# Two denominator groups a job, one ones product per norm in the FFN stages, and conv modulation weights outside the weight ring

## The reference

```python
for i in range(2):
    mod = silu(c) @ mod_w[i] + mod_b[i]              # six parts: shift, scale, gate, twice
    u = rms_norm(h, g) * (1 + scale) + shift
    y = conv_mixer(u) if i == 0 else attention(u)    # i==0: (b * conv3(c * x)) @ w_out
    h = h + gate * rms_norm(y, g)
    u = rms_norm(h, g) * (1 + scale2) + shift2
    f = (silu(conv3(u @ w_up)[g]) * conv3(u @ w_up)[up]) @ w_down
    h = h + gate2 * rms_norm(f, g)
```

## Time and profile before

| | |
|---|---|
| median of 3 runs | 2504.2 us (2503.1 to 2543.51) |
| the profiled execution | 2507.53 us; its slowest core, core 6, spans 2506.5 us |
| spans of the cores | 2487.3 to 2506.5 us |
| PE busy | 2361.9 us, 94% of the span |
| DVE, ACT, POOL busy | 1573.4, 1348.9 and 1193.9 us |
| DMA moved | 231.93 MB written, mean 93 GB/s |
| mean granted clock of the PE | 0.988 to 0.995 by core |

### The profile page before, as it was taken

One profiled execution on the slowest core, in us unless ns is written; L12 is line 12 of the kernel. 1 busy time (PEld: TensorE's weight loads), 2 busy tenths in 40 slices (PEclk: granted clock), 3 DMA queues, 4 the chain that ended last, 5 costly groups with the idle time before them and its releaser, 6 DMA issues.

```text
span 2506.5 us, 37361 instructions; the slowest of 8 cores (2487.3 to 2506.5 us)
## 1 busy us (share of the span) xinstructions
PE 2361.9 (94%) x12748; PEld 1089.5 (43%) x12993; DVE 1573.4 (63%) x1747; ACT 1348.9 (54%) x1851; POOL 1193.9 (48%) x1106
## 2 busy tenths in 40 slices
PE   4898989999999999999889999999999999999998
PEld 1443444444444444444444333333344444444446
DVE  2447765766286818762776788397497547747742
ACT  3342524544258535444787888899554435534433
POOL 1355555744367548465363343320364455546434
PEclk9999999999999999999999999999999999999999
DMA  9738564464477545635334400200354465539621
GB/s 187 160 69 171 121 110 80 85 109 78 83 160 146 112 80 101 110 69 100 64 59 96 128 14 9 30 1 1 68 101 83 76 138 116 106 70 181 112 47 68
DMA packets 72458, 231.93 MB, mean 93 GB/s; under 512 B 8016, under 2 KB 13648, under 8 KB 71760
## 3 DMA queue, kind: packets, MB, share of 16 engines
q0 software_dynamic: 48512, 170.55, 40.3%
q1 hardware_dynamic: 23760, 58.97, 7.3%
HBM read 370.65 MB, written 29.36 MB: 160 GB/s over the span
## 4 chain that ended last, share of the span: by engine, by line
PE 78%; issue 6%; DMA 6%; DVE 5%; ACT 3%; POOL 2%; DVEq 0%; ACTq 0%; SPq 0%; POOLq 0%
PE ps L671 38%; PE ps L604 22%; PE ps L1025 5%; PE ps L1035 5%; PE ps L875 3%; DMA wr<-win 2%; DVE ra L703 2%; DMA ra<-modw 1%; POOL rs L489 1%; PE ps L1052 1%; DMA h<-x_in 1%; PE ps L495 1%; ACT wr L102 1%; ACT yb L102 1%; PE ps L685 1%
## 5 line engine op out<-in xcount | busy, mean ns | idle before, releaser
L671 PE MATMUL ps<-u,wr 128*128 128x512 bf16 x5199 | 1173.2, 381 | 30.1 <-DMA wr<-win 16.5
L671 PEld LDWEIGHTS ps<-u,wr 128*128 128x128 bf16 x5328 | 513.6, 98 | 633.5 <-issue 41.1
L703 DVE SCALAR_TENSOR_TENSOR ev<-ps,par,ev 128x1023 f32<-128x1023 f32 (+1 forms) x336 | 428.4, 1281 | 160.6 <-ACT ev L102 129.2
L604 PE MATMUL ps<-ra,wr 128*128 128x512 bf16 (+1 forms) x2292 | 509.2, 379 | 15.4 <-ACT sqb L102 3.7
L604 PEld LDWEIGHTS ps<-ra,wr 128*128 128x128 bf16 x2338 | 228.8, 98 | 289.5 <-issue 25.3
L102 ACT ACTIVATE wr<-ps 128x1024 bf16<-128x1024 f32 (+1 forms) x352 | 329.3, 985 | 46.0 <-PE ps L1025 44.5
L102 ACT ACTIVATE ev<-ps,par 128x1024 f32<-128x1024 f32 x168 | 186.8, 1112 | 224.5 <-PE ps L671 221.2
L703 DVE SCALAR_TENSOR_TENSOR ra<-ps,par,ra 128x1023 f32<-128x1023 f32 (+1 forms) x192 | 243.4, 1278 | 37.2 <-ACT ra L102 24.8
L789 POOL TENSOR_TENSOR ra<-ev 128x1023 bf16<-128x1023 f32 (+1 forms) x84 | 199.1, 2370 | 141.9 <-ACT ev L102 70.0
L489 POOL TENSOR_TENSOR rs<-rs,sqb 128x512 f32<-128x512 f32 (+1 forms) x125 | 181.2, 1457 | 125.8 <-ACT sqb L102 124.4
L1035 PE MATMUL ps<-wr,ra 128*128 128x512 bf16 x622 | 188.8, 380 | 5.8 <-DVE ra L1062 2.6
(11 more groups left out here) (185 smaller groups left out, 2691.4 us busy)
## 6 DMA issues: line engine op xcount, KB each, us to landing
wr<-wup POOLq DMA_DIRECT2D x132, 512.0 KB, 6.2
wr<-wdn POOLq DMA_DIRECT2D x41, 704.0 KB, 6.5
wr<-modw POOLq DMA_DIRECT2D x40, 512.0 KB, 6.5
wr<-win POOLq DMA_DIRECT2D x24, 768.0 KB, 9.5
h_mem<-h SPq DMA_DIRECT2D x24, 512.0 KB, 5.5
h<-h_mem SPq DMA_DIRECT2D x24, 512.0 KB, 5.7
h_out<-h SPq DMA_DIRECT2D x40, 256.0 KB, 5.4
h<-x_in SPq DMA_DIRECT2D x16, 512.0 KB, 10.2
```

The source lines that it names most:

```text
L604: ins = e.matmul(bank(b, n), w3[:, k, :], rhs(k), start=(k == 0), stop=(k == nk - 1))
L671: ins = e.matmul(bank(b + ct), lhs_fn(kc), ub.ap[:, kc, ct * 512:ct * 512 + 512], start=(kc == 0), stop=(kc == KC - 1))
L703: P.dve(lambda e, ro=ro, zi=zi, w=w: e.scalar_tensor_tensor(out=ro, in0=zi, scalar=w, in1=ro, op0=ALU.mult, op1=ALU.add), 1024, rd + wr, w ...
```

## The change

Three edits, and what follows from them for the order.

1. **Denominators.** `denominators` runs twice a job, after items 9 and 19, on five sums each, where it ran five times on two. The pair sums no longer overwrite an exp tile; they go to a ring of eight tiles of their own. For S0 that ring is the upper half of `h0` (chunks 4 to 7 of the h buffer that P's residual and its stores to memory use just before), for S1 the first 16 KB of `ra_t`. With that, `wo_out` of S0 uses the lower half of `h0` for one of its two output buffers in place of the start of `ra_t`, and `A` (L321) learns to name the h tiles.
2. **Ones products.** In the FFN stages the norms and the out phases use `groups=(0,)`: all eight squares are added on POOL and one ones product sums them. Before, it was (0, 7), and `range(KC)` for the norm of S1 at L1235. `final_out` keeps (0, 7) for its last part. Conv and attention stages are unchanged.
3. **Modulation weights.** Parts 2 to 5 of layer 0 are loaded by `load_apart` by turns into three blocks of `ra_t` (bytes 32768 to 45055), which the conv stages do not use otherwise; the ring holds only win and wout tiles there. Those of layer 1 stay in the ring.
4. The planner sees the new list; nothing in its costs changes.

```diff
 def A(name, lo, hi):
+    if name[0] == "h":
+        return [(name, b // 2, b % 2) for b in range(lo // 2048, (hi + 2047) // 2048)]
     return [(name, b) for b in range(lo // 1024, (hi + 1023) // 1024)]
...
-wpos = {"b": 0, "lim": WR}
+wpos = {"b": 0, "lim": WR, "m": 0}
...
-def mod_gen(l, parts):
+def load_apart(src):
+    i = wpos["m"] = (wpos["m"] + 1) % 3
+    ap, keys = ra_t[:, (8 + i) * 2048:(9 + i) * 2048], A("ra", (8 + i) * 4096, (9 + i) * 4096)
+    P.dma("pool", ap, src, 128 * 4096, writes=keys)
+    return ap, keys
+
+def mod_gen(l, parts, apart=False):
     for part in parts:
         for bi in range(4):
-            mod_mm(l, part, bi, *load_w(modw[l, part * 4 + bi], KC * 256))
+            src = modw[l, part * 4 + bi]
+            mod_mm(l, part, bi, *(load_apart(src) if apart else load_w(src, KC * 256)))
...
-      lambda _, o, ok: P.act(n, "ps", pk(b), ok, o, bank(b, n), AF.Square), (0, 7))
+      lambda _, o, ok: P.act(n, "ps", pk(b), ok, o, bank(b, n), AF.Square), groups)
...
-      sb, m, (2, 3, 0)[i], i == 0 and m < 2)
+      sb, m, (2, 3, 0)[i], i == 0 and m < 2, (0, 7) if i == 2 else (0,))
...
-def attend(U, qbuf, osbs):
+def attend(U, qbuf, osbs, sums):
     ob, nk, npt = 4, 20, 8
+    st, sn, s0 = sums
...
-    P.dve(lambda e: e.tensor_tensor(out=I.pt, in0=s, in1=I.pt, op=ALU.add), 512, sk + I.pk, I.pk, sh=True)
-    J.sums.append((I.pt, I.pk, c))
+    cnt["sum"] = (cnt["sum"] + 1) % 8
+    o = s0 + cnt["sum"] * 2048
+    t, tk = st[:, o // 2:o // 2 + 1024], A(sn, o, o + 2048)
+    P.dve(lambda e: e.tensor_tensor(out=t, in0=s, in1=I.pt, op=ALU.add), 512, sk + I.pk, tk, sh=True)
+    J.sums.append((t, tk, c))
 def denominators(J):
-    nb, J.sums = J.sums[:2], J.sums[2:]
+    nb, J.sums = J.sums[:5], J.sums[5:]
...
-    for lag, cs, fn in ((5, (3, 7, 11, 15, 19), denominators), (6, (19,), recip), (10, (19,), norm_o)):
+    for lag, cs, fn in ((5, (9, 19), denominators), (6, (19,), recip), (10, (19,), norm_o)):
...
-    return out_phase(U, l, 3, NCF, lambda m: wdn[l, m], dn, dnk, ybs, BO, **kw)
+    return out_phase(U, l, 3, NCF, lambda m: wdn[l, m], dn, dnk, ybs, BO, groups=(0,), **kw)
...
-      (mod_gen(0, [2]), 1, 0.8), (load_h(S1, x_in, 1), 0, 0.5), stats=S1)
+      (mod_gen(0, [2], True), 1, 0.8), (load_h(S1, x_in, 1), 0, 0.5), stats=S1)
...
-at(P.prio + 60.0, lambda: norm(S1, 1, 0, 0, None, bk=7, groups=range(KC), on="act"), False)
-stage(ffn_in(PU, 0, UU, False), ffn_out(PU, 0), [lambda: norm(S0, 0, 2, 3, UU)],
+at(P.prio + 60.0, lambda: norm(S1, 1, 0, 0, None, bk=7, groups=(0,), on="act"), False)
+stage(ffn_in(PU, 0, UU, False), ffn_out(PU, 0), [lambda: norm(S0, 0, 2, 3, UU, groups=(0,))],
...
-g = attend(S0, UU, [(yb_t, "yb", 12288)])
+g = attend(S0, UU, [(yb_t, "yb", 12288)], (h_t[0].bitcast(BF16), "h0", 16384))
...
-g = attend(S1, UE, [(raf, "ra", 36864), (raf, "ra", 40960)])
+g = attend(S1, UE, [(raf, "ra", 36864), (raf, "ra", 40960)], (ra_t, "ra", 0))
...
-run(wo_out(S0, UU, [(yb_t, "yb", 0), (raf, "ra", 0)]))
+run(wo_out(S0, UU, [(yb_t, "yb", 0), (h_t[0], "h0", 0)]))
```

More of the change, by code:

```diff
@@ L608, in block, with out_phase @@
             sumsq(m, sb, n, rs_t[:, ai * 512:ai * 512 + n], [("rs", ai)],
-                  lambda _, o, ok: P.act(n, "ps", pk(b), ok, o, bank(b, n), AF.Square), (0, 7))
-        def out_phase(U, l, gi, nk, wsrc, rhs_fn, rkeys, ybs, banks, **kw):
+                  lambda _, o, ok: P.act(n, "ps", pk(b), ok, o, bank(b, n), AF.Square), groups)
+        def out_phase(U, l, gi, nk, wsrc, rhs_fn, rkeys, ybs, banks, groups=(0, 7), **kw):
             bi = 0
@@ L623, in out_phase @@
                           yb[:, y0 // 4 + m * 512:y0 // 4 + (m + 1) * 512], A(ybn, y0 + m * 2048, y0 + m * 2048 + 2048),
-                          6 + ct, m, 2 + ct, m < 2)
+                          6 + ct, m, 2 + ct, m < 2, groups)
                     yield
@@ L951, in load_tab @@
                 P.dma("sp", tab[:, a, :], rope[a, :, U.ui * 1024:U.ui * 1024 + 1024], 128 * 4096, writes=TA[a])
-        cnt = {"pt": 0, "set": 0, "o": 0, "rc": 0}
+        cnt = {"pt": 0, "set": 0, "o": 0, "rc": 0, "sum": 0}
         rcp_t = yb_t[:, 3072:4096]
@@ L1267, in build_program @@
         at(P.prio + 10.0, lambda: norm_halo(1, 2, 3), False)
-        stage(ffn_in(S0, 1, UU, True, 24.0), ffn_out(S0, 1), [lambda: norm(S1, 1, 2, 3, UU)], (mod_gen(1, [5]), 4, 3.0), lead=4.0)
-        stage(ffn_in(S1, 1, UU, False), ffn_out(S1, 1), [lambda: norm(PU, 1, 2, 3, UU)], (load_h(PU, h_mem, 1), 6, 1.5), lead=4.0)
+        stage(ffn_in(S0, 1, UU, True, 24.0), ffn_out(S0, 1), [lambda: norm(S1, 1, 2, 3, UU, groups=(0,))], (mod_gen(1, [5]), 4, 3.0), lead=4.0)
+        stage(ffn_in(S1, 1, UU, False), ffn_out(S1, 1), [lambda: norm(PU, 1, 2, 3, UU, groups=(0,))], (load_h(PU, h_mem, 1), 6, 1.5), lead=4.0)
         run(ffn_in(PU, 1, UU, False))
```

10 lines of the change are left out of this document (5 added, 5 removed).

## The result

The kernel after the change takes 2515.7 us, median of 20 runs, against 2504.0 for 20 runs of the kernel before. Five of the first and one of the second were slow runs, those of the first with one die at a lower granted clock; without them the medians are 2512.1 and 2503.9 us, and every ratio in this text is taken without such runs. It is 1.0042 here, 95% interval 1.0025 to 1.0058, about 10.5 us more. 2480 was forecast, and the time is outside the range of 2464 to 2500. The profiled execution took 2512.1 us; its slowest core, core 1, spans 2511.0.

The account below looks back on a forecast made before the run. The PE was taken to set the time nearly everywhere; 18 + 6 + 2.5 = 26.5 us off the profiled 2507.5 gives 2481.0, or 2477.7 at the median, said as 2480 with a little kept back; range 2464 to 2500.

Parts of the forecast that it names:

- I charge nothing for that since no PE work of that stretch waits on anything queued behind them: Start of the kernel: two more modulation loads, behind the win loads in POOL's queue, were to cost 0 us.
- The first term, 18: Conv stages, part 1: modulation weights apart let win loads go earlier, giving 18 us, bounds 8 to 26.
- At 73.1 the load that went at 89.9 could go, and it would land long before 95: First conv stage: a win load could go one tile, about 10.4 us of PE work, earlier.
- What each of the six waits gives back: Conv stages, PE waits for win, 16.5 us: first gives 12.8 with clock, second 3, other four 2.3.
- The conv waits stay: Rival, conv stages: loads short of bandwidth, not ring space, land as late as before; 2494 us, chance 0.20.
- 5.1 us of clock loss at the first wait: First conv wait for win: lower granted clock in two slices around it costs 1.5 + 3.6 us more.
- Each missing 0.01 of a 10 us slice costs 0.1 us: Slices around the conv waits: rule that turns a lower granted clock into lost time.
- forecast at 6: Norms and out phases: 36 ones products fewer save 7.6 us, less one 1.5 us wait; bounds 2 to 7.6.
- forecast at 9 from the PE, 7.5 after ACT, less 5 for the stores: Latents' attention: two denominator groups save PE time, ACT lets 7.5 arrive, late first sums cost 5; net 2.5.
- The forecast's own two readings were 0.82 and 1.03: Attention: PE time in us of a five-set denominator group, by the trace or if each set pays its weight load.
- Ahead of it ACT has 5% of room, so most but not all of the 9 arrives: 7.5: Latents' attention: ACT's exps take 0.97 us each, so of 9 us PE time saved 7.5 arrives.
- Slower than before, by POOL's adds: Rival, out phases and norms: every last POOL add gates a ones product, 24 of them; 2514 us, chance 0.08.

Follow-up runs that it names:

- idle loads: Kernel before with three more loads of modulation blocks at the start that nothing reads, ring unchanged: ratio 1.0021.
- pacing the same loads: Kernel after with each apart load held until the program has reached the present conv product: ratio 0.9944, 2490.0 to 2492.1 us.
- one block ahead: Kernel after with its apart loads held to the conv products, each modulation block issued before the products of the block ahead of it: ratio 0.9977.
- one group: Kernel before with a single denominator group a job, the other eight pair sums left out, so for timing only: ratio 0.993.
- ring kernel with job 0 in place: Kernel after with modulation weights back in the ring and S0's first job keeping its sums in place in five groups: ratio 0.9971.
- ring kernel: Kernel after with its modulation weights back in the ring, denominators and ones products as changed: ratio 0.9966.

## Why the prediction was wrong

**Part 1, the sentence that failed** is "I charge nothing for that since no PE work of that stretch waits on anything queued behind them". I looked behind the extra loads in POOL's queue only. SP's x_in loads stand in no queue behind them, but share the DMA engines with them, and the PE's work depends on them through ACT's order: squares of the next unit's h ahead of the conv's own scaling. Runs show each link: idle loads delay x_in and the out phase (to 10.0 us and by 6.2 us, though two later win loads have a share in that), pacing the same loads brings x_in to 5.8 us, the out phase from 157.5 to 148.3 and the ratio from 1.0042 to 0.9944.

**The first term, 18, was mis-sized as well.** The step "At 73.1 the load that went at 89.9 could go, and it would land long before 95" was right as to the queue: the win waits went. But "What each of the six waits gives back" took the bandwidth as free. Even with the pacing the conv stages gain 3.9 us (431.1 against 435.0), not 18, and the ones products of these stages are in that. What had been waited for as win is waited for as modw (13.8 us paced, 14.4 one block ahead). On core 1 before, the first 110 us run at a DMA share of 0.90 and 185 GB/s on average, where the best slice of 10 us reaches 181 and the start 193: there is little room to bring everything earlier. That was the rival *The conv waits stay* in its cause (short of bandwidth, not of ring space), which I gave 0.20. Its time, 2494, missed, since it too let no wait grow. I had cited in its favour the slices at 0.99, and against it only that one load was held by its queue. Both were true. Two readings behind the 18 were off as well. The 16.5 us are those of the slowest core; by core the waits for win before are 10.1 to 16.8 us. And the 5.1 us of clock loss at the first wait count a low clock while the PE stood still (see the clock below); under matmuls it was 2.1, which makes the first item 9.8 and the sum 15.

**What was to show it.** Waits for win under 5 us: yes. No conv slice at 0.64: the lowest is at 0.67. PE idle in the conv stretch near 22 us: no, 45. L495 with 36 products fewer: yes, 110 weight loads of ones for 146. L1065 in 32 groups of 20, 0.8 us each: yes (0.73). A PE pause of 2 to 7 us ahead of the qkv of S1: 1.5. PE waits for ACT's exps as the most common of the attention: yes (5.8 us in 13 waits, before 2.2 in 6), and that was listed as a sign of being wrong.

**The clock** fell behind the new pauses as behind the old. But the forecast, "Each missing 0.01 of a 10 us slice costs 0.1 us", is too dear: a low clock costs only while matmuls run. Shorter stretches tell the two apart, before (core 6) and after (core 1):

```profile
97.00:103.00 6.00, 0.01 (x1) 0.14 (x3) 3.80 (x3) 1.90 (x4) 1.67 (x2) 0.50 1.01 205
103.00:107.00 4.00, 4.00 (x10) 1.50 (x10) 0.00 (x0) 1.20 (x2) 1.27 (x2) 0.50 1.00 153
```
```profile
107.00:112.00 5.00, 4.93 (x12) 1.75 (x13) 1.40 (x3) 1.81 (x3) 1.66 (x2) 0.50 1.03 192
...
121.00:126.00 5.00, 5.00 (x13) 1.76 (x12) 3.10 (x3) 1.97 (x5) 2.94 (x4) 0.50 0.64 107
```

Of the 5.1 us, 3.0 lay in the pause itself, and the 4.1 us up to 107.1 at half the clock cost 2.1. The two new pauses of 6.8 and 7.5 us are followed by 5.1 and 5.3 us at half the clock, 5.2 us in all: 19.5 us together, against 7.7 + 2.1 + 4.2 + 1.7 = 15.7 for the two waits for win on core 6.

**Part 2** was forecast at 6, from 36 products at 0.215 less one wait. Alone it measures 0.998, 5 us (2 to 8). The place is another than the sum has it: 26 of the 36 products lie in the FFN stages of layer 0 (5.6 us), which gained 2.3 to 8.0 us in the kernels with this part (those on the chip with the lower clock left out), and the other 10 behind the attention (2.1 us), where the kernel after gained 0.5. The added POOL work is there (402.95 us busy from 480 to 1160, before 372.34) and hidden: of the PE's waits for an add only the one of 7.5 us is longer than 1.8.

**Part 3** was forecast at 9 from the PE, 7.5 after ACT, less 5 for the stores. The PE's own cost is right; around one group after:

```profile
1642.66 0.59 PE L1045 MATMUL ps<-wr,ra 128*128 128x512 bf16 x2
1643.19 0.73 PE L1065 MATMUL ps<-ra,ones_h 128*32 128x256 bf16 x20
1643.85 0.60 PE L1035 MATMUL ps<-ev,ra 128*128 128x512 bf16 x2
```

From the value pair at 1642.66 it is 1.19 to the next scores, less 0.43 for the pair: 0.76 us a group of five sets (forecast 0.82). The forecast's own two readings were 0.82 and 1.03. The second was by the Trainium skill, TensorE: Matmul & The Clock Gate, Part 3: Packing small matmuls, as the forecast read it, and the trace speaks against that reading: three more sets cost (0.76 - 0.43) / 3 = 0.11 each, about their 256 columns. So the PE is spared 16 x (5 x 0.43 - 2 x 0.76) = 10 us. Jobs 2 to 16 got 4.2 us shorter in all (382.5 to 378.3). The step that failed is "Ahead of it ACT has 5% of room, so most but not all of the 9 arrives: 7.5". The 5% is a mean; ACT's room lies around the denominator groups, and between them ACT already is the pace. After, between two groups (core 1), and before with its five (core 6):

```profile
1644.55 9.65 ACT L102 ACTIVATE wr<-ps 128x1024 bf16<-128x1024 f32 x10 [0.55 <-PE ps L1035]
1654.76 7.99 ACT L102 ACTIVATE wr<-ps 128x1024 bf16<-128x1024 f32 x8 [0.55 <-PE ps L1035]
```
```profile
1640.67 3.89 ACT L102 ACTIVATE wr<-ps 128x1024 bf16<-128x1024 f32 x4 [0.23 <-PE ps L1025]
1644.79 4.10 ACT L102 ACTIVATE wr<-ps 128x1024 bf16<-128x1024 f32 x4 [0.22 <-PE ps L1025]
```

Ten exps run back to back at 0.965 each, an item of the PE is 0.86. A short group's wait of 0.22 us is partly made good by exps already queued; a long group costs ACT 0.55 in one piece. Five times 0.22 is 1.1 us a job and two times 0.55 also 1.1: what ACT loses to the groups is the same before and after. The whole idle time of ACT in two plain jobs of S1 (13 and 14, counted from 0) says the same: 1.7 us each before, 1.6 and 1.9 after, 0.9 with one group, and the jobs last 21.1, 20.9 to 21.2, and 20.2 us. The run with one group agrees in kind (0.64 of the saved time arrives). That a job's length follows ACT's gaps so closely is my reading of these rows; no run changed the exps alone.

The stores cost 1.5 us up to the qkv products and not 5, since they landed in 2.6 to 4.9 us, not in 6.5. Job 0 as a whole is 3.4 us longer than before (1.7 to 2.0 in the kernels with part 3 and the ring); 1.7 of it is lower clock, as shown above.

The forecast had no term for a third thing. Before, the PE stood at the start of S1's output product, behind the last job (core 6):

```profile
PE ps L604 <- DMA wr<-wo: 2.7, 1, 2.7
```

After, this wait is gone, and that out phase takes 31.4 us, not 33.2. With it the latents' attention is 3.5 us shorter. Part 3 was forecast at 2.5 net and came near that, but by luck: its terms were 7.5 and -5, and 4.2, -3.4 and some 2 at the end were measured, which leaves the terms short of the stretch by about a microsecond.

**The rival *Slower than before, by POOL's adds*** gave 2514, close to what was measured, and is not what happened. Its mechanism was a wait for the last add in the FFN's norms; the one large wait for an add, 7.5 us, is at 120.7 in the first conv stage, and that add had itself waited 10.26 us for a square of x_in.

**As a whole**, the parts 2 and 3 were forecast at 8.5 us and gave 0.9966, 8.5 (5 to 12). The agreement is luck in part, as the terms of part 3 show. The error is part 1: a gain of 18 forecast, a loss of 12 to 19 measured.

**A better kernel than both** came out of it: apart loads that are paced, with both other parts. It measured 0.9944 (14 us less than before). Beside it ran the ring kernel with job 0 in place, and 2490.0 to 2492.1 us for the paced one stand against 2495.3 to 2498.2: 6.4 us less in the medians, of which 2.5 are in the latents' attention (456.0 against 458.5), where job 0 differs. So the paced apart loads are worth some 4 us over the ring. A variant with almost the same milestones, one block ahead, gave 0.9977 beside other runs of before, which is no better than the ring kernel's 0.9966; why it is worse than 0.9944 no run tells.

## What to carry to other kernels

A shared ring of buffers is also a rate limiter: who gives a stream of loads its own buffers lets it run ahead, and must say what else is in flight then, on every DMA queue, and which engine has an operation in its order that waits for it. Before calling an early transfer free, add up the bytes up to the point in question; at a DMA share near 1 an earlier load is another load made later. And where two engines are within 5% on average, look at the timeline between the events that are to be thinned out: the other engine may already be the pace there.
